# Block form with seven products for the first four tiles of the output projection of a two-layer decoder step

## What is computed

```python
def mixer_layer(x, ...):
    xn = rmsnorm(x, ln_g)
    proj = xn @ w_in
    q, k, v, z_a, x_b, z_b, g_a, g_b = jnp.split(proj, SPLIT_IDX, axis=-1)
    ...
    merged = jax.nn.sigmoid(g_a) * (o_a @ w_a) + jax.nn.sigmoid(g_b) * (o_b @ w_b)
    return x + merged @ w_o, S_new, conv_new, h_last
```

## Time and profile before

| | before |
|---|---|
| median of 3 runs | 1903.36 us (1902.87 to 1903.52) |
| the profiled execution: its own time, its span | 1904.28 us, 1902.4 us |
| TensorE busy | 1879.9 us, 12984 matmuls |
| vector engine busy | 1262.3 us |
| scalar engine busy | 805.4 us |
| granted TensorE clock, mean | 0.999 |

### The profile page before, as it was taken

The page is one execution under the profiler, slowest core; times in us unless marked ns, Lnnn a source line. Parts: engine busy times, 40 slices in busy tenths (PEclk is TensorE's granted clock), DMA queues, the critical chain, the costliest instruction groups (busy, mean ns, idle before and its releaser), DMA issues.

```text
span 1902.4 us, 32236 instructions
## 1 busy us (share of the span) xinstructions
PE 1879.9 (99%) x12984; PEld 1762.1 (93%) x12984; DVE 1262.3 (66%) x2144; ACT 805.4 (42%) x1293; POOL 284.4 (15%) x399
## 2 busy tenths in 40 slices
PE   8999999999999999999999999999999999999998
PEld 7899898898899999999998988988988999999997
DVE  8775665665766877864487656657557678878445
ACT  5432332423437776542344323234124377766323
POOL 2220120120232200100022201202102422001000
PEclk9999999999999999999999999999999999999999
DMA  6434544453443432643354445534544533327332
GB/s 219 134 120 165 168 140 131 161 183 110 144 157 91 112 99 91 157 121 115 104 173 157 141 126 177 172 114 150 167 120 144 165 101 107 98 83 193 103 122 78
DMA packets 114786, 257.48 MB, mean 135 GB/s; under 512 B 11822, under 2 KB 52254, under 8 KB 114510
## 3 DMA queue, kind: packets, MB, share of 16 engines
q1 hardware_dynamic: 84350, 156.00, 26.4%
q0 software_dynamic: 30144, 99.41, 16.6%
q10 hardware_dynamic: 144, 0.00, 0.0%
HBM read 196.55 MB, written 49.12 MB: 129 GB/s over the span
## 4 chain that ended last, share of the span: by engine, by line
PE 86%; DVE 5%; ACT 3%; DMA 2%; DVEq 1%; issue 1%; ACTq 1%; SPq 0%
PE bank L1944 20%; PE bank L1946 20%; PE bank L1945 20%; PE bank L2014 4%; PE bank L2015 4%; PE bank L2016 4%; DMA w_raw<-in_w_units 1%; PE last L2032 1%; PE last L2014 1%; PE last L2016 1%; PE last L2015 1%; PE bank L2282 1%; PE bank L2285 1%; PE bank L2284 1%; PE sums L2147 1%
## 5 line engine op out<-in xcount | busy, mean ns | idle before, releaser
L1944 PE MATMUL bank<-xn_hi,w_hi 128*128 128x296 f32 (+1 forms) x2176 | 651.9, 300 | 0.4 <-DVE w_lo L531 0.2
L1946 PE MATMUL bank<-xn_lo,w_hi 128*128 128x296 f32 (+1 forms) x2176 | 647.6, 298 | 0.0
L1945 PE MATMUL bank<-xn_hi,w_lo 128*128 128x296 f32 (+1 forms) x2176 | 646.8, 297 | 0.0
L1944 PEld LDWEIGHTS bank<-xn_hi,w_hi 128*128 128x128 f32 x2176 | 409.9, 188 | 6.9 <-issue 4.3
L1945 PEld LDWEIGHTS bank<-xn_hi,w_lo 128*128 128x128 f32 x2176 | 410.5, 189 | 1.0
L1946 PEld LDWEIGHTS bank<-xn_lo,w_hi 128*128 128x128 f32 x2176 | 409.5, 188 | 0.0
L524 ACT ACTIVATE w_hi<-w_raw 128x1024 fp32r<-128x1024 f32 x229 | 240.7, 1055 | 357.8 <-DMA w_raw<-in_w_units 355.3
L531 DVE TENSOR_TENSOR w_lo<-w_raw,w_hi 128x1024 fp32r<-128x1024 f32 x229 | 280.6, 1228 | 93.3 <-ACT w_hi L524 86.5
L1944 PE MATMUL bank<-oa_hi,w_hi 128*128 128x296 f32 (+1 forms) x512 | 154.0, 301 | 0.0
L1945 PE MATMUL bank<-oa_hi,w_lo 128*128 128x296 f32 (+1 forms) x512 | 152.1, 297 | 0.0
L1946 PE MATMUL bank<-oa_lo,w_hi 128*128 128x296 f32 (+1 forms) x512 | 152.0, 297 | 0.0
(11 more groups left out here) (331 smaller groups left out, 3540.9 us busy)
## 6 DMA issues: line engine op xcount, KB each, us to landing
w_raw<-in_w_units SPq DMA_DIRECT2D x199, 512.0 KB, 3.7
S<-in_state_ret POOLq DMA_DIRECT2D x64, 512.0 KB, 4.8
out_ret_s<-S POOLq DMA_DIRECT2D x64, 512.0 KB, 6.2
w_raw<-in_w_units SPq DMA_DIRECT2D x122, 256.0 KB, 3.2
vst<-v_scr SPq DMA_DIRECT2D x8, 512.0 KB, 4.1
out_ret_p<-Sp POOLq DMA_DIRECT2D x8, 512.0 KB, 5.7
w_raw<-in_w_units POOLq DMA_DIRECT2D x16, 256.0 KB, 4.8
v_scr<-vtok_hi SPq DMA_DIRECT2D x16, 160.0 KB
```

What stands on the lines that cost most here:

```text
L1944: pe.matmul(ps, w_hi[:, slot, cols], x_hi, start=first, stop=False)
L1945: pe.matmul(ps, w_lo[:, slot, cols], x_hi, start=False, stop=False)
L1946: return pe.matmul(ps, w_hi[:, slot, cols], x_lo, start=False, stop=last)
```

## The change

The first four tiles of the output projection are done as two pairs in the 7-product form, in each layer; tiles 4 to 7 stay as they were (the job table's phase O has one pass of four tiles now). The constants:

```diff
+                                      ("O", 1, 4, four)):
         out[name] = Phase(at, passes, units, jobs)
...
+OUT_PAIRS = 2
+LAYER_PAIRS = TILE_PAIRS + OUT_PAIRS
 PRODUCTS = 7
-PART_UNITS = TILE_PAIRS * PRODUCTS
```

```diff
+                def of_merged(m):
+
+                    if m < 4:
+                        dve.tensor_tensor(diff[:, m, 0:wide], acc[:, m, a0:b0], acc[:, m, a1:b1], SUB).then_inc(right_ready, 1)
+                        return
+                    k = m - 4
+                    dve.tensor_tensor(edge[:, k, 0:wide], acc[:, m, a1:b1], acc[:, k, a1:b1], SUB).then_inc(right_ready, 1)
+                    dve.drain()
+                    dve.scalar_tensor_tensor(mix2[:, k, 0:wide], acc[:, k, a0:b0], -1.0, edge[:, k, 0:wide], MUL, SUB)\
+                       .then_inc(right_ready, 1)
+                    dve.drain()
+                    dve.scalar_tensor_tensor(last_right[:, k, 0:wide], mix2[:, k, 0:wide], -1.0, acc[:, m, a0:b0], MUL, SUB)\
+                       .then_inc(right_ready, 1)
```

TensorE takes the last branch tile in another order (four k-steps for both halves, then eight for both), which frees its first unit earlier, and then the two pairs:

```diff
+                    for n, early in ((0, True), (1, True), (0, False), (1, False)) if m == KT - 1 else ((0, None), (1, None)):
...
+                at = l * RIGHTS + 4
+                for t in range(OUT_PAIRS):
+                    two, before, x, y, z = TILE_PAIRS + t, (l * OUT_PAIRS + t) * PRODUCTS, bank[t], bank[2], bank[3]
+                    x, y, z = x[:, 0:wide], y[:, 0:wide], z[:, 0:wide]
+                    wait_bank(pe, "O", l, 0, (("proj", 0), t))
+                    product(two, A11, x, xn_hi[:, 0:4, a0:b0], xn_lo[:, 0:4, a0:b0], True,
+                            mgl_ready, l * KT + 1, 1)
+                    if t == 0:
+                        wait_bank(pe, "O", l, 0, (("proj", 1), 0))
+                    else:
+                        pe.wait_ge(x_taken, before - PRODUCTS + S4 + 1)
+                    product(two, S1, y, diff_hi[:, :, 0:wide], diff_lo[:, :, 0:wide], True, right_lo, at + 1, 1)
+                    pe.wait_ge(x_taken, before + A11 + 1)
+                    product(two, S2, x, mix2_hi[:, :, 0:wide], mix2_lo[:, :, 0:wide], False, right_lo, at + 5, 3)
+                    if t == 0:
+                        wait_bank(pe, "O", l, 0, (("proj", 1), 1))
+                    else:
+                        pe.wait_ge(x_taken, before - PRODUCTS + A12 + 1)
+                    product(two, A12, z, xn_hi[:, 4:KT, a0:b0], xn_lo[:, 4:KT, a0:b0], True, mgl_ready, l * KT + 5, 1)
+                    pe.wait_ge(x_taken, before + S2 + 1)
+                    product(two, S3, x, edge_hi[:, :, 0:wide], edge_lo[:, :, 0:wide], False, right_lo, at + 6, 3)
+                    pe.wait_ge(x_taken, before + S1 + 1)
+                    product(two, S4, y, xn_hi[:, 4:KT, a1:b1], xn_lo[:, 4:KT, a1:b1], False)
+                    pe.wait_ge(x_taken, before + S3 + 1)
+                    product(two, A22, x, last_hi[:, :, 0:wide], last_lo[:, :, 0:wide], False, right_lo, at + 7, 3)
+                if l + 1 == DEPTH:
+                    break
+                project("O", l, 0, ("proj", 0), 0, (0,))
+                pe.wait_ge(x_taken, (l + 1) * OUT_PAIRS * PRODUCTS)
+                project("O", l, 0, ("proj", 0), 0, (1,))
+                for i in range(1, 4):
+                    project("O", l, 0, ("proj", i), i)
```

S2, S3, S4 and A22 accumulate in a bank that the vector engine must have read out before (x_taken), and the second pair's S1 and A12 start in banks of the first. That reading adds the bank straight to acc, with a factor of 0.5 or -0.5, once x is back there:

```diff
+                def taken(two, product, ps, tile, part, scale, first_of=None, last_of=False):
+
+                    a, b = cut(l)[part]
+                    if first_of is not None:
+                        dve.wait_ge(x_again[tile % 4], l * 32 + 32)
+                    dve.wait_ge(part_done, l * PART_UNITS + two * PRODUCTS + product + 1)
+                    dve.scalar_tensor_tensor(acc[:, tile, a:b], ps[:, 0:wide], scale, acc[:, tile, a:b], MUL, ADD)\
+                       .then_inc(x_taken, 1)
+                    dve.drain()
+                    if last_of:
```

The vector engine's order for the first pair, behind the branch stage's loop:

```diff
+                two, x = TILE_PAIRS, bank[0]
+                of_merged_low(4 + 3 * 3 + 1, 3)
+                taken(two, A11, x, 0, 0, 0.5, True)
+                part_low(two, A12)
+                low_merged(KT - 1)
+                taken(two, S1, bank[2], 1, 1, -0.5, True)
+                of_merged_low(4 + 3 * 3 + 2, 3)
+                taken(two, S2, x, 0, 1, 0.5)
+                part_low(two, S3)
+                of_merged_low(4 + 3 * 3 + 3, 3)
+                taken(two, A12, bank[3], 0, 0, 0.5)
+                part_low(two, S4)
+                part_low(two, A22)
+                taken(two, S3, x, 1, 1, -0.5)
+                part_low(two + 1, A11)
+                taken(two, S4, bank[2], 0, 1, 0.5, None, True)
+                part_add(two + 1, S2, S1)
+                part_low(two + 1, S1)
+                taken(two, A22, x, 1, 0, -0.5, None, True)
+                part_add(two + 1, S4, S2)
```

GpSimd's queue reloads tile k and tile k + 4 of x separately now, and interleaves that with the additions for S1 and S3:

```diff
+
+                    pool.wait_ge(mgl_ready, l * KT + k + 5)
+                    apart(pool)
+                    for m in (k, k + 4):
+                        pool.dma_start(acc[:, m, :], (x_in if l == 0 else x_scr[l - 1])[:, m * T:m * T + T])\
+                            .then_inc(x_again[k], 16)
+
                 for two in range(TILE_PAIRS):
-                    for part, (m, k), landed in ((S1, (1, 1), s1_in), (S3, (0, 0), s3_in)):
-                        n = two * PRODUCTS + part
-                        pool.wait_ge(part_in[part_slot(l, n)], part_arrived(l, n))
-                        pool.dma_start(part_of(w_raw, l, n), w_units[l * STORED_LAYER + B_AT + 2 * two + m]
-                                       [:, k * 4 * P:k * 4 * P + 4 * P], accum_op=ADD).then_inc(landed[two % 2], 16)
-                for two in range(TILE_PAIRS):
-                    pool.wait_ge(mgl_ready, l * KT + 2 * two + 2)
-                    apart(pool)
-                    pool.dma_start(acc[:, 2 * two:2 * two + 2, :].rearrange("p k t -> p (k t)"),
-                                   (x_in if l == 0 else x_scr[l - 1])[:, 2 * two * T:(2 * two + 2) * T])\
-                        .then_inc(x_again[two], 16)
+                    add_part(two, S1)
+                    add_part(two, S3)
+                load_again(0)
+                add_part(TILE_PAIRS, S1)
+                load_again(1)
+                load_again(2)
+                add_part(TILE_PAIRS, S3)
+                load_again(3)
+                for two in range(TILE_PAIRS + 1, LAYER_PAIRS):
+                    add_part(two, S1)
+                    add_part(two, S3)
```

More of the change, by code:

```diff
@@ new lines, in _ @@
+                two = TILE_PAIRS
+                part_high(two, S3)
+                part_high(two, S4)
+                part_high(two, A22)
+                part_high(two + 1, A11)
+                part_high(two + 1, S1)
+                part_high(two + 1, S2)
+                part_high(two + 1, A12)
+                two += 1
+                part_high(two, S3)
+                part_high(two, S4)
+                part_high(two, A22)
+                tile_high(0)
+                split_hi(act, "O", l, 0, 0 - AHEAD)
@@ L1859, in _ @@
                         if n == 1 and m >= 1:
[L1860 removed]
+                            next_low(done)
                             done += 1
@@ new lines, in _ @@
+                part_low(two, S4)
[7 more added lines that the diff above has]
+                part_add(two + 1, S4, S2)
+                part_low(two + 1, S2)
+                two, x = two + 1, bank[1]
+                taken(two, A11, x, 2, 0, 0.5, True)
@@ new lines, in _ @@
+                part_low(two, A12)
+                taken(two, S1, bank[2], 3, 1, -0.5, True)
+                tile_low(0)
+                taken(two, S2, x, 2, 1, 0.5)
+                part_low(two, S3)
+                part_low(two, S4)
+                taken(two, A12, bank[3], 2, 0, 0.5)
+                part_low(two, A22)
+                taken(two, S3, x, 3, 1, -0.5)
+                split_lo(dve, "O", l, 0, 0 - AHEAD)
+                taken(two, S4, bank[2], 2, 1, 0.5, None, True)
+                split_lo(dve, "O", l, 0, 1 - AHEAD)
@@ L1905, in result @@
+                for i in range(4):
+                    for n in range(2):
+                        new_x(i, n).then_inc(freed("O", (("proj", i), n)), 1)
+                    dve.drain().then_inc(x_ready, 1)
+                    if i == 0:
+                        tile_low(2)
+                        tile_low(3)
+                    split_lo(dve, "O", l, 0, i)
+                    for k in ((), (4, 5), (6,), (7,))[i]:
+                        tile_low(k)
             def result(n, k):
@@ L2274, in _, with product @@
                         gates(it, g, 2)
-                def product(two, part, ps, x_hi, x_lo, start):
+                def product(two, part, ps, x_hi, x_lo, start, ready=None, count=0, step=0):
                     n = two * PRODUCTS + part
```

275 lines of the change are left out of this document (177 added, 98 removed).

## The result

The changed kernel takes 1909.57 us (median of 6 runs, 1908.75 to 1912.43) against 1903.44 for the kernel before (6 runs beside it, 1902.52 to 1906.54): ratio 1.0035, 95% interval 1.0024 to 1.0046. It is 6.1 us slower; the forecast was 6.9 us slower (1910.3). The profiled execution, 1912.43 us with a span of 1910.3, is the slowest of the six, so its absolute times are read as differences within a stage.

A forecast was written before the change was run, and what follows sets the result against it. TensorE's matmuls bound the kernel (busy 1879.9 of 1902.4 us). Per layer 2.7 + 3.7 + 0.5 - 3.2 = +3.7, two layers +7.4, less 0.5: 1903.4 + 6.9 = 1910.3 us, range 1904.7 to 1917.

The forecast's parts named there:

- 48 matmuls fewer: Output projection, two tile pairs in each of two layers: block form needs 84 matmuls for 96, saving 3.2 us a layer.
- branch stage: Stage before the output projection: added vector engine and ACT work is covered by waiting there, so 0 us.
- wait A: TensorE before the first pair's third product, S2, held until the vector engine takes out A11: 2.7 us a layer.
- wait B: TensorE before the first pair's S3, whose accumulating DMA queues behind reloads on GpSimd: 3.7 us a layer, 1.6 to 5.1.
- wait C: Second pair of the output projection, TensorE waiting for the heavily loaded vector engine: 0.5 us a layer, 0 to 1.7.
- start of layer 1: Existing 0.56 us wait for the sum of squares; finished tiles come earlier, so up to 0.5 us is won.
- With 7.4: Before S3: time from GpSimd's issue of the accumulation to TensorE's start, from the g_B stage's 7.15 and 7.60 us.
- S2 and A12, from 913.4, end at 913.4 + 24 x 0.136: First pair, layer 0: these two products, 24 matmuls at 0.136 us each, end at 916.7, before S3 could start at 920.4.
- The granted clock at 1.00 in both places: Expected sign in the changed profile: TensorE's clock stays full at the idle times before S2 and before S3.
- The rival that had it fall: Clock halves in the wait before S3, slowing matmuls behind it: +3 to +10 us, 1915 likely; chance 0.10.
- this load is covered: SP's half-unit loads in the output projection: with the last branch tile's new order, S2's parts are not delayed.
- Wrong if S3's idle time is under 1 us: Sign that would refute the forecast: TensorE idle under 1 us before S3's first matmul, where 2 to 5 was expected.

The follow-up runs named there:

- lows_before_eviction: Changed kernel with the vector engine making tile 6's xn_lo and its blocks' low halves before the last branch tile's first eviction: 1905.71 us.
- both_queues: Changed kernel with the vector engine's order behind the last eviction and GpSimd's order (accumulations ahead of reloads) both rearranged, finished tile 0 later: 1904.08 us.
- s3_sum_first: Changed kernel with the first pair's accumulating DMA for S3 put ahead of the reload of tiles 2 and 6 on GpSimd's queue: 1907.25 us.
- changed_again: The changed kernel run once more with no edit: 1909.83 us, ratio 1.0037 to the kernel before.
- array_kept_busy: Changed kernel with 20 matmuls whose result nobody reads, on TensorE between S1 and S2 of the first pair: 1912.15 us.
- first_tile_later: Changed kernel with the vector engine's work on the first finished tile moved behind the second pair's last taking: 1907.91 us.
- plain_last_tile: Changed kernel with the last branch tile back in its old order on TensorE, all of half 0, then half 1: 1920.44 us.
- two_reloads_late: both_queues with the reloads of tiles 6 and 7 moved behind the second pair's accumulation for S3: 1901.87 us, ratio 0.9998 to the kernel before.

## Why the prediction was right

Right in sign and size: 1910.3 forecast, 1909.57 measured. The cause, two queues' orders, is as forecast too; the closeness of the number is in part luck, as three terms were off and their errors nearly cancel. By its steps, layer 0 / layer 1, each gap less one spacing of 0.14:

| step | predicted | measured |
|---|---|---|
| 48 matmuls fewer | -3.2 a layer | -3.2 / -3.2 (24 x the spacing) |
| branch stage | 0 | 0; TensorE has no gap up to the end of S1 |
| wait A | 2.7 | 2.6 / 2.6 |
| clock behind A | 0 | 1.5 / 1.3 |
| wait B | 3.7 | 0.8 / 1.6 |
| wait C | 0.5 (0 to 1.7) | 1.8 / 0.6 |
| start of layer 1 | -0.5 once | -0.4 |

**Wait A** is right to 0.1 us. The chain from the last eviction to the start of S2 was to take 913.4 - 907.64 = 5.8 us and took 914.12 - 908.49 = 5.6; lows_before_eviction and both_queues show that it is DVE's order.

**Wait B** has the right cause (s3_sum_first) and the right time of issue: 913.0 - 907.45 = 5.55 us into the stage predicted, 913.84 - 908.29 = 5.55 measured. Two terms of it failed. "With 7.4", the way from issue to TensorE in the earlier trace rows, was too long: 6.0 and 6.5 were measured. And "S2 and A12, from 913.4, end at 913.4 + 24 x 0.136" held the full clock: at half speed they ended 1.5 us later, inside the wait. S3 started 11.56 us into the stage, for 12.95 predicted. The changed profile gives these DMAs a median of 4.7 us to landing, so the estimate of 2.6 us by the Trainium skill, "DMA: Bandwidth & Descriptors", "Anatomy of one DMA — SWDGE (gpsimd) path", does not hold here either.

**The clock.** "The granted clock at 1.00 in both places" is wrong. The rival that had it fall was right in kind, and wrong in place (behind A in both layers of the changed kernel; behind B in layer 1 of changed_again) and in price: 3 to 10 us was for a fall that nothing hides. In the changed kernel the fall fills the time until S3 is ready. Behind B it cost 0.8 us in layer 1 of array_kept_busy, and in its layer 0 wait C took it up. The prediction read from the end of the run that the clock fell 2 to 4 us after the last matmul, and asked about wait B alone, although its own wait A, 2.7 us, was in that range too; behind A it fell, after 2.4 us idle.

**Wait C** was priced by analogy with the g_B stage, at the low end. In layer 0 it was just over its upper bound. The list there, "seven takings, four part low halves, three unit splits and two finished tiles", counted DVE's work and not that one of the items waits for ACT: the step that failed is taking a queue's load for its delay. first_tile_later shows it for the larger part.

**The last tile's order** was left at "this load is covered", which is right; that it is worth 10.6 us was not seen.

**Its own signs of being wrong.** "Wrong if S3's idle time is under 1 us": in layer 0 it was 0.67 us, so this sign came true there while the total stayed right. The clock did show 0.50, behind S2 and not behind S3's wait. TensorE did not wait in the branch.

The errors of B (-2.5 a layer), the clock (+1.4) and C (+0.7) nearly cancel, so the total is closer than its terms, and that is luck. Measured terms give +3.1 in layer 0 and +2.9 in layer 1, the stage lengths +3.3 and +3.3.

## What to carry to other kernels

When an engine's products are cut in number, cost the chain that feeds the first dependent one: list what stands in each queue between the last producer and that product, the DMA queue too, and ask of every item what it waits for itself. Put what can be made early ahead of the wait, and what nobody needs yet behind it, DMAs included: these reorderings took the loss of 6.9 us to 1.2, and with two more DMAs moved, to none that can be measured. No order tried made the kernel faster than before. A wait taken away in one place is handed on to the next late landing, so look at the stage's length and not at the one gap.

## What the runs showed of the hardware

- TensorE's granted clock fell to half (0.50, matmuls 0.245 us apart) behind idle times of 2.4 us and more between matmuls; 12 to 14 matmuls ran so in the changed kernel, 24 in layer 0 of lows_before_eviction. It did not fall behind every one: in layer 1 of s3_sum_first 2.89 us idle, in layer 1 of changed_again 2.39, were followed by a clock of 1.00. Behind pauses of up to 2.08 us (plain_last_tile, second pair's S3) it stayed at 1.00 in the output stages of all these kernels. The Trainium skill ("TensorE: Matmul & The Clock Gate", "Part 1: The HAM clock gate") has an idle array go to 1.2 GHz; the traces agree that it does, though not at every pause of this size.
- A load of 256 KB on SyncE's queue landed in 2.5 us (median of three) beside one reload and one accumulation on GpSimd's queue, and in 6.5 us (median of two) beside four reloads of 296 KB, all in both_queues; in two_reloads_late, beside two reloads and one accumulation, in 5.5 us (median of two).
